# Two layers of a hybrid decoder: the head-pair loop reordered on every engine, and the suffix sums of the softplus folded on VectorE and ScalarE

## The reference

```python
h = _rmsnorm(x, mix_norm_g[l])
a_b, a_c, a_x, s_u, s_v, q, k, v, gates = _split_cols(h @ w_in[l])
ya = _short_conv(a_b, a_c, a_x, conv_w[l], conv_b[l])     # B * conv3(C * x)
yb = _sgu(s_u, s_v, ...)                                  # gelu(u) * (tril(W) v + b)
yc = _stick_breaking(qh, kh, vh)                          # 8 heads of 64, q and k normalised
merged = sum_i sigmoid(gate_i) * (y_i @ w_branch_out[l][i])
x = x + merged @ w_o[l]
x = x + (silu(g) * up) @ w_down[l]                        # of rmsnorm(x)
```

```python
log_1m = jnp.where(mask, jax.nn.log_sigmoid(-z), 0.0)     # = -softplus(z)
after = lax.cumsum(log_1m, axis=3, reverse=True) - log_1m
a = jnp.where(mask, jnp.exp(jax.nn.log_sigmoid(z) + after), 0.0)
out = a @ v
```

## Time and profile before

| | |
|---|---|
| median of 3 runs | 1672.76 us (1672.59 to 1673.02) |
| profiled execution: time | 1673.66 us |
| profiled execution: span | 1671.9 us |
| PE (TensorE matmul) busy | 1662.9 us, 7608 matmuls |
| DVE (VectorE) busy | 949.4 us, 1172 instructions |
| ACT (ScalarE) busy | 752.4 us, 1059 instructions |
| POOL (GpSimd) busy | 190.6 us, 177 instructions |
| HBM | 155.26 MB read, 94 GB/s over the span |

### The profile page before, as it was taken

The page is one execution under the profiler, slowest core; times in us unless marked ns, Lnnn a source line. Parts: engine busy times, 40 slices in busy tenths (PEclk is TensorE's granted clock), DMA queues, the critical chain, the costliest instruction groups (busy, mean ns, idle before and its releaser), DMA issues.

```text
span 1671.9 us, 22070 instructions
## 1 busy us (share of the span) xinstructions
PE 1662.9 (99%) x7608; PEld 1386.7 (83%) x7608; DVE 949.4 (57%) x1172; ACT 752.4 (45%) x1059; POOL 190.6 (11%) x177
## 2 busy tenths in 40 slices
PE   8999999999999999999999999999999999999999
PEld 7888888888888888888888888888888888888887
DVE  6887876545554434434549877765555544344344
ACT  6677676333353222222456777763333432232231
POOL 0333311000020000000133233200001200000000
PEclk9999999999999999999999999999999999999999
DMA  5222222233233233233343122222323232232233
GB/s 190 84 81 88 88 76 82 89 100 100 94 101 100 89 101 100 89 101 100 113 127 101 64 88 88 88 70 96 98 90 110 89 101 96 93 100 100 89 100 126
DMA packets 49153, 162.20 MB, mean 97 GB/s; under 512 B 5712, under 2 KB 5968, under 8 KB 49104
## 3 DMA queue, kind: packets, MB, share of 16 engines
q1 hardware_dynamic: 46512, 157.08, 28.8%
q10 hardware_dynamic: 2592, 4.49, 0.7%
HBM read 155.26 MB, written 2.10 MB: 94 GB/s over the span
## 4 chain that ended last, share of the span: by engine, by line
PE 94%; DVE 2%; ACT 1%; DVEq 1%; POOLq 0%; POOL 0%; issue 0%; DMA 0%; ACTq 0%
PE bank L504 28%; PE bank L505 28%; PE bank L508 28%; PE z L577 2%; PE z L505 1%; PE z L508 1%; PE z L504 1%; PE z L550 1%; PE misc L593 1%; PE misc L591 1%; PE z L551 1%; DVE S L1321 0%; DMA par<-in_params 0%; PE bank L632 0%; DVE N L1198 0%
## 5 line engine op out<-in xcount | busy, mean ns | idle before, releaser
L504 PE MATMUL bank<-xg_hi,w_hi 128*128 128x512 f32 x1584 | 620.0, 391 | 0.0
L505 PE MATMUL bank<-xg_lo,w_hi 128*128 128x512 f32 x1584 | 616.8, 389 | 0.0
L818 ACT ACTIVATE w_hi<-raw 128x1024 fp32r<-128x1024 f32 (+1 forms) x294 | 303.5, 1035 | 483.8 <-DMA raw<-in_w_units 483.0
L1186 DVE TENSOR_TENSOR w_lo<-raw,w_hi 128x1024 fp32r<-128x1024 f32 (+1 forms) x294 | 371.2, 1265 | 42.1 <-ACT w_hi L818 21.8
L508 PE MATMUL bank<-xg_hi,w_lo 128*128 128x512 f32 x1584 | 391.7, 389 | 0.0
L508 PEld LDWEIGHTS bank<-xg_hi,w_lo 128*128 128x128 f32 x1584 | 297.4, 188 | 61.7
L504 PEld LDWEIGHTS bank<-xg_hi,w_hi 128*128 128x128 f32 x1584 | 297.5, 188 | 61.0
L505 PEld LDWEIGHTS bank<-xg_lo,w_hi 128*128 128x128 f32 x1584 | 297.5, 188 | 60.6
L1191 DVE TENSOR_TENSOR S<-bank,rstd 128x512 f32<-128x512 f32 x152 | 104.9, 690 | 267.0 <-PE bank L508 266.4
L504 PE MATMUL bank<-mid_hi,w_hi 128*128 128x512 f32 x474 | 184.6, 390 | 0.0
L505 PE MATMUL bank<-mid_lo,w_hi 128*128 128x512 f32 x474 | 184.4, 389 | 0.0
(11 more groups left out here) (200 smaller groups left out, 1675.9 us busy)
## 6 DMA issues: line engine op xcount, KB each, us to landing
raw<-in_w_units SPq DMA_DIRECT2D x278, 512.0 KB, 3.3
raw<-in_w_units SPq DMA_DIRECT2D x19, 256.0 KB, 2.9
xT<-in_x SPq DMA_DIRECT2D x8, 256.0 KB, 6.7
mix_hi<-yb_hi ACTq DMA_DIRECT2D x8, 256.0 KB, 2.3
mix_lo<-yb_lo ACTq DMA_DIRECT2D x8, 256.0 KB, 2.4
out_x<-xT SPq DMA_DIRECT2D x7, 256.0 KB, 3.9
ln_g<-in_sgu_ln_g SPq DMA_DIRECT2D x2, 256.0 KB, 4.2
ln_b<-in_sgu_ln_b SPq DMA_DIRECT2D x2, 256.0 KB, 5.0
```

Of the source, the lines that this page charges most:

```text
L504: mm(dst[:, :], wh[:, k0 + k, :], his[k], start=(k % per == 0), stop=False)
L505: mm(dst[:, :], wh[:, k0 + k, :], los[k], start=False, stop=False)
L818: af(w_hi[at.slot(c)][:, 0:kc, :], raw[at.slot(c)][:, 0:kc, :], ACT.Copy).then_inc(hi_done, 1)
L1186: tt(w[:, 0:kc, :], r[:, 0:kc, :], h[:, 0:kc, :].bitcast(F32), ALU.subtract).then_inc(lo_done, 1)
```

## The change

It has five parts.

- `cumulate` sums the softplus of the later blocks first and runs the square of -1 over that sum once. `fold_halves` (ScalarE) copies the lower 64 partitions' 768 columns up, `fold_sums` (VectorE, three dependent additions of 64 x 768, 64 x 128 and 64 x 256) adds them to the upper 64 and forms the suffix sums, `fold_round` (ScalarE) and `fold_lo` (VectorE) write the high half into partitions 0 to 63 and the low half into 64 to 127 of `fold_hl`. `suffix` on POOL goes.
- The squares of q and k move from POOL to ScalarE (`head_square`, two passes) and VectorE (`square_lo`) in the pairs. POOL keeps `k_rest` alone there.
- The pairs are reordered: the scores and the softplus of a pair's first head, and its unit 0, stand at the end of the pair before (ahead of the loop for the first one). `head_squares` of k comes ahead of the second head's scores, and `attend` one unit later.
- At the start SyncE loads the first half of unit 0, which stood on ScalarE's queue.
- One option of the program's frame, the scratch for dynamic DMAs, is set to 4096.

```diff
-                        for s, u in parts:
-                            terms = [(neg_tri, s, S_AT[i], i)]
-                            if i == 0:
-                                terms.append((neg_ones, s, S_AT[1], 1))
-                            if i < 2:
-                                terms.append((neg_ones, u, 0, 2))
-                            if i == 2:
-                                terms.append((neg_ones, s, S_AT[3], 3))
...
+                        for s in (s_hi, s_lo):
+                            last = mm(z[g][:, at:at + width], neg_tri[:, :], s[:, S_AT[i]:S_AT[i] + width],
+                                      start=False, stop=(s is s_lo and i == 3), skip_group_check=True)
+                        if i < 3:
+                            last = mm(z[g][:, at + P:at + width], neg_ones[:, :], fold_hl[:, later[i]],
+                                      start=False, stop=True, skip_group_check=True)
...
+            def fold_halves(h3):
+
+                act.wait_ge(sp_ok, h3 + 3)
+                af(fold[0:HD, :], t_s[HD:P, T:1280], ACT.Copy).then_inc(fold_up, 1)
+
+            def fold_round(nth):
+
+                act.wait_ge(fold_sum, nth + 1)
+                act.sem_inc(passed, 1)
+                af(fold_hl[0:HD, :], fold[0:HD, :], ACT.Copy).then_inc(fold_hi, 1)
...
+            def head_square(n_raw, src):
+
+                act.wait_ge(qk_raw, n_raw)
+                act.sem_inc(passed, 1)
+                af(S2[:, :], src[:, :], ACT.Square)
+                af(sq_hi[:, :], src[:, :], ACT.Square).then_inc(qk_sq_hi, 1)
...
+            def fold_sums(nth):
+
+                half = slice(0, HD)
+                dve.wait_ge(fold_up, nth + 1)
+                dve.sem_inc(passed, 1)
+                tt(fold[half, :], fold[half, :], t_s[half, T:1280], ALU.add)
+                dve.drain()
+                tt(fold[half, 5 * P:], fold[half, 5 * P:], fold[half, 3 * P:4 * P], ALU.add)
+                dve.drain()
+                tt(fold[half, P:3 * P], fold[half, P:3 * P], fold[half, 4 * P:], ALU.add)
+                dve.drain()
+                dve.sem_inc(fold_sum, 1)
...
+                    softplus_sum(h3 + 6)
+                    fold_sums(heads + 2)
+                    scaled(pl["A"](j + 1), 0, N0[:, :])
+                    dve.drain()
+                    dve.sem_inc(v_raw, 1)
+                    yc_add(heads + 1, 1)
```

More of the change, by code:

```diff
@@ L68 @@
 M_P, M_PAIR, M_PAIR_LAST = 2, 6, 3
+M_T, M_SQ, M_SK, M_E0, M_MIX, M_E1 = range(6)
+M_LAST_E0, M_LAST_MIX = 1, 2
 M_LAYER = M_P + (PAIRS - 1) * M_PAIR + M_PAIR_LAST + 1
@@ L1001, in pair @@
                     h3 = l * 24 + j * 6
+                    heads = l * 8 + j * 2
                     pairs = l * PAIRS + j
@@ L1084, in pair @@
                     ln_exp_table()
-                    yc_half(m0 + 5)
-                    yc_round(l * 8 + (j * 2 + 1), j, 1)
+                    act.wait_ge(a_lo, h3 + 6)
+                    softplus_logs(h3 + 6)
+                    fold_halves(h3 + 6)
+                    yc_half(m0 + M_E1)
+                    softplus_hi(h3 + 6)
+                    yc_round(heads + 1, j, 1)
+                    fold_round(heads + 2)
                 ln_exp_table()
+                softplus_logs(l * 24)
+                fold_halves(l * 24)
+                softplus_hi(l * 24)
+                fold_round(l * 8)
                 with act.Fori(0, PAIRS - 1) as j:
@@ L1429, in v_rest @@
                         dve.sem_inc(misc_free, 1)
-                    scaled(at, 0, N0[:, :])
-                    dve.drain()
-                    dve.sem_inc(v_raw, 1)
-                    softplus_sum(h3)
-                    softplus_lo(h3)
+                    fold_lo(heads)
+                    split_lo(at, 3)
                     if last:
-                        split_lo(at, 3)
                         scaled(at, 1, S0[:, :])
+                        v_rest()
                         split_lo(at, 4)
-                        v_rest()
                         scaled(at, 2, S1[:, :])
@@ L1449, in pair @@
                         split_lo(at, 6)
-                        yc_add(l * 8 + j * 2, 0)
+                        convolution()
                         softplus_sum(h3 + 3)
-                        yc_rest(l * 8 + j * 2, j, 0)
-                        convolution()
+                        fold_sums(heads + 1)
+                        yc_add(heads, 0)
                         softplus_lo(h3 + 3)
+                        yc_rest(heads, j, 0)
                         scaled(at, 4, S2[:, :])
@@ L1458, in pair @@
                         dve.sem_inc(u_raw, 1)
+                        split_lo(at, 7)
                         ya_rest()
-                        split_lo(at, 7)
-                        mixed(m0 + 2, j1)
+                        fold_lo(heads + 1)
+                        mixed(m0 + M_LAST_MIX, j1)
                         with_u(pairs)
@@ L1470, in pair @@
                     dve.sem_inc(qk_raw, 1)
-                    split_lo(at, 3)
+                    v_rest()
+                    square_lo(l * 6 + j * 2)
                     split_lo(at, 4)
-                    v_rest()
                     dve.wait_ge(k_ok, pairs + 1)
@@ L1526, in with_u @@
                     tt(N0[:, :], N0[:, :], S2[:, :], ALU.mult).then_inc(yb_pre, 1)
+                softplus_sum(l * 24)
+                fold_sums(l * 8)
+                scaled(pl["A"](0), 0, N0[:, :])
+                dve.drain()
+                dve.sem_inc(v_raw, 1)
+                softplus_lo(l * 24)
                 with dve.Fori(0, PAIRS - 1) as j:
```

148 lines of the change are left out of this document (75 added, 73 removed).

## The result

The changed kernel takes 1713.68 us (median of 4 runs, 1712.98 to 1714.14) beside 1672.89 of the kernel before: ratio 1.0239, 95% interval 1.0226 to 1.0252. It is 40.8 us slower. The direction and the place were as predicted, the size was not: 1699 was forecast, at most 1708. The profiled execution took 1713.6 us with a span of 1711.9, so the comparison with the trace of before is 1713.6 - 1673.66 = +39.9 us.

A forecast was written before the change was run, and what follows sets the result against it. TensorE, busy 99%, was taken as the bound, with longer ScalarE and VectorE chains now making it wait. 13.3 us a layer, +26.6 in two, took 1673.66 to 1700.3 profiled, 1699 as median; range 1680 to 1708.

The forecast's parts named there:

- Matmuls removed: In `cumulate`: 1280 columns fewer, 0.64 us less and 1.63 us per head; sixteen heads give -10.2 us.
- Entry: Ahead of the loop's first transposes: v ready only at 84.9, so TensorE waits 4.0 us, once a layer.
- The pass of the loop: Three passes a layer: 60.3 us each through ScalarE and VectorE, 3.0, 3.8 and 3.8 us longer than before.
- the slow value: VectorE's convolution beside POOL's `k_rest`: 5.0 us, its first step 1.61; the fast value would save 0.9.
- The wait at the transposes: Late in each loop pass: v out and `misc` free at 54.3, TensorE there at 52.2, waiting 2.2 us.
- The chain as a whole: One loop pass: ScalarE and VectorE steps in sequence make 60.3 us, where TensorE alone needs 55.4.
- The last pair and the start: Last pair has slack and gains its two `cumulate`, -1.3 us; start between -0.7 and +0.3, taken as 0.
- The sum: Whole kernel: 4.0 + 3.0 + 3.8 + 3.8 - 1.3 = 13.3 us a layer, +26.6 for two.
- The range: Whole kernel: 1680 to 1708 us, leaving out the faster and unchanged cases and the clock's far end.
- the clock's rival: Entry's wait lowers TensorE's clock, 2 us more each, perhaps some in the loop: 1703, at most 1712; chance 0.2.

The follow-up runs named there:

- the reordered version: Changed kernel with v, misc and exponentials moved earlier, `ya_round` behind `yb_round`, `mixed` ahead of `q_rest`, and u, `with_u`, `attention_lo` at the convolution: 1668.81 us.
- the last version: Against the kernel at 1668.81 us, on VectorE the q to be squared is taken out ahead of a weight unit's low half: 1667.66 us.

## Why the prediction was wrong

- **Matmuls removed.** Right: 1.62 us a head for 1.63.
- **Entry.** The wait was forecast at 4.0 and is 4.1; the transposes come 4.2 later for it. The step that failed is that the sum put nothing for the clock behind this wait, and left it to a rival. 7.54 - 5.93 = 1.6 and 8.69 - 5.93 = 2.8 make 4.4 us for the two layers, about the 2 us a layer that the rival named. Filling the wait gave 3.7 back. (The Trainium skill, TensorE: Matmul & The Clock Gate, Part 1, has idleness return the engine to the half clock: the entry agrees.)
- **The pass of the loop.** This is the term that was mis-sized most: forecast 3.0 + 3.8 + 3.8 us over before in a layer, measured 4.2 + 5.4 + 5.5 (61.71, 62.11, 62.19 against 57.5, 56.7, 56.7). That is 4.5 more a layer, 8.9 in all. The steps, counted from the second pair's `cumulate` at 153.70:

| step | forecast | measured |
|---|---|---|
| first exponentials start | 0.78 | 1.42 |
| `rms_chain` of k starts | 10.0 | 10.58 |
| softplus summed | 18.0 | 18.5 |
| `misc` free (`yc_add` ends) | 22.1 | 22.8 |
| convolution starts | 30.4 | 31.1 |
| convolution ends | 35.4 | 36.7 |
| exponentials again, start | 36.95 | 38.45 |
| TensorE's `scores` start | 38.3 | 40.05 |

Of the 1.75 us by which `scores` is late, 0.64 arose at the first step: ScalarE still had a square of q and a weight split ahead of the exponentials. The forecast had seen some of this (0.4 late from the second pass on) and put only 0.2 of it into the pass. In the convolution arose 0.65. For this I had taken 5.0, "the slow value", from a row in which `k_rest` ended ahead of the second step (174.95 against 175.73). Shifted by a microsecond, it also covers that step, 1.20 for 0.55. The run without `k_rest` shows both steps at their short values and a chain that is shorter by the convolution's 1.54. From `scores` to the next transposes the chain was 16.1, as forecast.

- **The wait at the transposes.** It was forecast at 2.2 us in each pass. It is 2.07 in the first, but 0.5 and 0.6 in the second and third, where the clock behind the wait at `scores`, also put at nothing, had made TensorE 1.6 us later. The pass is not longer for it, so the time does not show this miss.
- **Hand-overs.** The rest of the 1.75, some 0.45 us a pass, lies in steps that each came a little later than their forecast. I have no run that isolates it.
- **The chain as a whole.** Right in kind, the waits are those of one chain through ScalarE and VectorE: moving `misc` and v ahead of the fold gave 17.8 us, the exponentials ahead of `ya_round` 8.1 with the clock kept up, and v first at the entry 6.4. These add up to 1713.7 - 17.8 - 8.1 - 6.4 = 1681.4, and the three together measured 1680.05.
- **The last pair and the start.** -1.2 for -1.3, and -0.7 in the profiled execution where 0 was taken; the start alone makes no measurable difference. The scratch option, costed at nothing, was never changed alone, but the reordered version has it too and runs at 1668.8.
- **The sum.** 26.6 + 8.9 (loop) + 4.4 (clock at the entry) + 0.4 (entry's wait) + 0.2 - 0.7 = 39.8, measured 39.9.
- **The range.** Its upper end, 1708, left out the far end of the clock's rival (1712), and the measured time lies beyond both, since the pass and the clock were missed together. Both misses have one sign: a chain of fifteen steps taken from their shortest gaps can be late at each and early at none, and each wait that grows can bring the clock's cost with it.
- **The fold itself** is not what is slow: with its order put right, the same operations run 4.8 us under the kernel before. What the whole change is worth in the best order tried is that much; the order it came with costs 45. In the old order, with the squares still on POOL, the fold alone cost 29 to 37 us: it needs an order made for it.

## What to carry to other kernels

When a chain through two engines is put before the bounding engine's next operand, look for what stands in their orders ahead of the instruction that releases it and doesn't belong to it (here `fold_halves` and `fold_sums` ahead of `misc` and v, `ya_round` ahead of the exponentials), and move that behind. In a forecast for a kernel like this one, give a wait of TensorE of 4 us a surcharge of 1.6 to 2.8 us for the clock and one of 2 to 3 us the chance of 1.6, and don't read an experiment that shifts waits without comparing the granted clock behind them. A row taken beside another engine's work holds only for that overlap; if the chain moves by a microsecond, it has to be laid out anew.

## What the runs showed of the hardware

- The granted clock behind waits of 3.9 to 4.1 us ahead of the transposes read 0.66 to 0.78 on the mean over the next unit, in each window shown, which cost 1.6 to 2.8 us; with the wait filled it read 1.00.
- Behind waits of 1.9 to 2.8 us it fell in some places and not in others: it fell behind four of the six waits of 2.0 to 2.2 us at the transposes in the run without `k_rest`, behind 2.19 us in the first layer of the reordered version, and behind 2.8 us ahead of `scores` in the changed kernel's second and third passes. It did not fall behind 2.07 us at the changed kernel's 147.72, behind 2.19 us in the second layer of the reordered version, behind 1.88 us in the last version, and behind 2.82 us in the changed kernel's first pass.
- VectorE beside POOL: a product of two SBUF tensors took 1.59 instead of 0.69 us, a `tensor_scalar` of one 1.20 instead of 0.55, the 64 x 768 subtraction 1.68 instead of 0.95, two 1024-column splits 4.02 instead of about 2.4. (The Trainium skill, GPSIMD Engine Reference, section 1 (Specifications), names instructions with two SBUF inputs or in a two-port mode as those that contend; the first and the last two agree, and for the `tensor_scalar` the trace doesn't show its mode.)
